# Early modulation groups as column strips, x loaded ahead of the parameter rows

## What is computed

```
cs = jax.nn.silu(c)
for l in range(DEPTH):
    mod = cs @ P['w_mod'][l] + P['b_mod'][l]            # (2, 1024) @ (1024, 6144)
    sh1, sc1, g1, sh2, sc2, g2 = jnp.split(mod[:, None, :], 6, axis=-1)
    hn = _rms_norm(x, P['norm_mix_g'][l]) * (1.0 + sc1) + sh1
    y = mixer(hn, ...)                                  # begins with hn @ w_in
    x = x + g1 * y
    hn = _rms_norm(x, P['norm_ffn_g'][l]) * (1.0 + sc2) + sh2
    x = x + g2 * _swiglu(hn, P['w_ffn_in'][l], P['w_ffn_out'][l])
y = _rms_norm(x, P['final_norm_g'])
```

## Time and profile before

| | us |
|---|---|
| median of three runs | 1574.86 (1574.68 to 1576.28) |
| the profiled execution | 1577.25 |
| its span, first to last instruction | 1575.7 |
| PE busy in the span | 1456.3 (92%) |
| first projection matmul starts | 80.4 |

### The profile page before, as it was taken

The page is one execution under the profiler, slowest core; times in us unless marked ns, Lnnn a source line. Parts: engine busy times, 40 slices in busy tenths (PEclk is TensorE's granted clock), DMA queues, the critical chain, the costliest instruction groups (busy, mean ns, idle before and its releaser), DMA issues.

```text
span 1575.7 us, 28758 instructions
## 1 busy us (share of the span) xinstructions
PE 1456.3 (92%) x11021; PEld 1387.6 (88%) x11021; DVE 911.6 (58%) x1644; ACT 511.2 (32%) x763; POOL 128.9 (8%) x150
## 2 busy tenths in 40 slices
PE   5789999996999999999949999996979999999997
PEld 4789899796999999999939888885979999999997
DVE  3566567648886788378674447655463333333344
ACT  2135444424222222222343335443232212222233
POOL 0000000001221122012000000000001100100100
PEclk9999999997999999999969899998989999999998
DMA  8324334342554455345212131230312323233222
GB/s 257 133 81 141 114 124 125 111 137 91 173 163 147 147 161 161 107 137 162 67 40 56 35 85 52 71 93 18 93 54 80 93 87 87 80 94 93 81 74 77
DMA packets 230317, 164.67 MB, mean 105 GB/s; under 512 B 9990, under 2 KB 216520, under 8 KB 230100
## 3 DMA queue, kind: packets, MB, share of 16 engines
q1 hardware_dynamic: 217636, 118.47, 25.9%
q0 software_dynamic: 12288, 44.85, 8.6%
q10 hardware_dynamic: 304, 0.10, 0.0%
HBM read 159.80 MB, written 3.60 MB: 104 GB/s over the span
## 4 chain that ended last, share of the span: by engine, by line
PE 74%; DVE 12%; ACT 6%; issue 4%; DMA 3%; SPq 1%; POOL 0%; DVEq 0%; ACTq 0%; POOLq 0%
PE ring L606 64%; PE core_j L444 2%; ACT weight_high L416 1%; DVE weight_low L421 1%; DMA weight_raw<-in_c_w_in 1%; DMA mixer_area<-in_x_sample 1%; PE core_j L546 1%; PE core_k L1315 1%; PE ring L2144 1%; PE core_j L517 1%; DVE norm_rstd L616 1%; DVE norm_step L614 1%; DMA weight_raw<-in_a_w_in 0%; PE core_k L1318 0%; DVE norm_step L613 0%
## 5 line engine op out<-in xcount | busy, mean ns | idle before, releaser
L606 PE MATMUL ring<-normed_high,weight_high 128*128 128x272 f32 x2128 | 455.2, 296 | 42.7 <-DVE normed_low L698 27.3
L606 PE MATMUL ring<-normed_high,weight_low 128*128 128x272 f32 x2128 | 446.9, 292 | 0.0
L606 PE MATMUL ring<-normed_low,weight_high 128*128 128x272 f32 x2128 | 445.9, 291 | 0.0
L606 PEld LDWEIGHTS ring<-normed_high,weight_high 128*128 128x128 f32 x2128 | 341.3, 193 | 53.8 <-issue 45.5
L606 PEld LDWEIGHTS ring<-normed_low,weight_high 128*128 128x128 f32 x2128 | 341.5, 192 | 0.0
L606 PEld LDWEIGHTS ring<-normed_high,weight_low 128*128 128x128 f32 x2128 | 339.4, 193 | 0.0
L421 DVE TENSOR_TENSOR weight_low<-weight_raw,weight_high 128x1024 fp32r<-128x1024 f32 x197 | 257.3, 1306 | 72.1 <-ACT weight_high L416 70.6
L416 ACT ACTIVATE weight_high<-weight_raw 128x1024 fp32r<-128x1024 f32 x197 | 206.8, 1050 | 180.1 <-PE ring L606 156.2
L606 PE MATMUL ring<-mixed_high,weight_high 128*128 128x272 f32 x960 | 204.0, 294 | 17.9 <-DVE mixed_low L1992 7.4
L606 PE MATMUL ring<-mixed_high,weight_low 128*128 128x272 f32 x960 | 201.3, 292 | 0.0
L606 PE MATMUL ring<-mixed_low,weight_high 128*128 128x272 f32 x960 | 200.6, 291 | 0.0
(11 more groups left out here) (384 smaller groups left out, 1257.2 us busy)
## 6 DMA issues: line engine op xcount, KB each, us to landing
weight_raw<-in_w_ffn_in SPq DMA_DIRECT2D x88, 512.0 KB, 3.7
mod_weight<-in_w_mod POOLq DMA_DIRECT2D x48, 512.0 KB, 4.2
mod_weight<-in_w_mod POOLq DMA_DIRECT2D x18, 1024.0 KB, 5.7
weight_raw<-in_w_ffn_out SPq DMA_DIRECT2D x32, 512.0 KB, 3.6
weight_raw<-in_a_w_in SPq DMA_DIRECT2D x24, 512.0 KB, 4.0
weight_raw<-in_c_w_in SPq DMA_DIRECT2D x20, 512.0 KB, 3.8
mixer_area<-in_w_mod SPq DMA_DIRECT2D x6, 1024.0 KB, 12.4
weight_raw<-in_w_ffn_out SPq DMA_DIRECT2D x16, 384.0 KB, 3.2
```

What stands on the lines that cost most here:

```text
L606: last = pe.matmul(PS[p.slot][:, half, 0:HALF], w[n.slot][:, k, :], x[:, k, half * HALF:(half + 1) * HALF], start=(k == 0 and w is WH and ...
```

## The change

1. SP issues x and x_sample directly behind the identity (which now brings the two selector columns along), and the nine parameter rows behind them. All eight early groups go through SP's queue, in the order 0, 4, 1, 5, 2, 6, 3, 7, the first two projection weights behind the second. POOL loads group 8 and on.
2. The eight early groups are made as strips, in pairs, two groups to a bank of 512 columns, two banks in turn (`early_rows`). ACT copies a pair's rows out (`early_copy`), PE folds them by four matmuls (`early_fold`), and DVE adds the biases pair by pair (`early_read`). One pair makes sh1 and sc1 of two feature tiles.
3. The strips of the last pair and its fold stand between contraction tiles of the first two projections. Group 8's strips stand behind these.
4. ACT squares x as it was loaded, token-major, with the sum along the row. The reciprocal root is taken on 128x5 numbers, and PE spreads it over the partitions by five matmuls. DVE copies the transposed x out.
5. The norm's gain is made pair by pair, and the tiles of a pair directly behind it (`norm_gain`, `norm_tile`). DVE's softplus stands behind all of them.
6. SP's loop over the heads is written out.

The diff, cut to its core:

```diff
+        MG_ORDER = (0, 4, 1, 5, 2, 6, 3, 7)
...
+        def early_rows(pe, i):
+
+            if i >= 2:
+                pe.wait_ge(s_mrc, 2 * (i - 1))
+            for e in (2 * i, 2 * i + 1):
+                pe.wait_ge(s_early[e % EARLY_BUFS], 16 * (e // EARLY_BUFS + 1))
+                rows_of(pe, EARLY[e % EARLY_BUFS], EPS_ROWS[i % 2][:, 2 * P * (e % 2):2 * P * (e % 2) + 2 * P])
+
+        def early_fold(pe, i):
+            pe.wait_ge(s_mrc, 2 * i + 2)
+            if i >= 2:
+                pe.wait_ge(s_mod, 2 * (i - 1))
+            for n in range(4):
+                mm = pe.matmul(EPS_COLS[i % 2][:, 2 * n:2 * n + 2], EROWS[i % 2][:, n * P:(n + 1) * P], FOLD,
+                               start=True, stop=True)
+            mm.then_inc(s_modu, 2)
+
+        def rows_of(pe, w, dst):
+
             for k in range(KD):
                 q = slice(32 * (k % 4), 32 * (k % 4) + 32)
-                mm = pe.matmul(MRPS[q], CSW[:, k, :], MW[:, k, :], start=(k < 4), stop=(k >= 4))
+                mm = pe.matmul(dst[q], CSW[:, k, :], w[:, k, :], start=(k < 4), stop=(k >= 4))
             mm.then_inc(s_mrows, 1)
...
         def _(sp):
...
-            with sp.Fori(0, HEADS) as h:
+            for h in range(HEADS):
...
         def _(pool):
-            load_mod(pool, 0, lambda: MG_DIRECT)
...
-            pool.wait_ge(s_modu, 1)
-            load_mod(pool, 0, lambda: MG_DIRECT + 1)
-            pool.wait_ge(s_direct, MG_DIRECT)
+            pool.wait_ge(s_mrows, MG_NORM - 2)
+            load_mod(pool, 0, lambda: MG_NORM)
+            pool.wait_ge(s_modu, MG_NORM)
             for a in (XB[:, 0:PAD], XB[:, TC + PAD - 1:TC + PAD], GW[0], GW[1]):
                 ins = pool.memset(a, 0.0)
             ins.then_inc(s_clear, 1)
-            pool.wait_ge(s_modu, MG_NORM - MG_DIRECT)
-            load_mod(pool, 0, lambda: MG_NORM)
...
         def _(pe):
...
+            early_rows(pe, 0)
+            pe.wait_ge(s_add, KD)
+            p = Turn(R_N0)
+            pe.wait_ge(s_free[p.slot], p.before)
+            for b in range(NB):
+                pe.matmul(PS[p.slot][:, 0, b * P:(b + 1) * P], NR[:, b:b + 1].to_broadcast([P, P]), IDENT,
+                          start=True, stop=True)
...
+            early_fold(pe, 0)
+            early_rows(pe, 1)
+            early_fold(pe, 1)
+            early_rows(pe, 2)
+            early_fold(pe, 2)
...
+            for k in (0, 1):
+                first_two(k)
+            early_rows(pe, 3)
+            for k in (2, 3):
+                first_two(k)
+            early_fold(pe, 3)
+            for k in (4, 5, 6, 7):
+                first_two(k)
             pe.wait_ge(s_mod, MG_NORM)
             mod_rows(pe, MG_NORM)
...
         def _(act):
...
+            early_copy(act, 0)
+            act.wait_ge(s_squ, 1)
+            p = Turn(R_N0)
+            st.add(act.activation(NR[:, 0:TP], PS[p.slot][:, 0, :], ACT.Copy))
+            act.activation(NR[:, TP:T], PS[p.slot][:, 1, 0:TS], ACT.Copy).then_inc(s_free[p.slot], 1)
+            early_copy(act, 1)
+            norm_high(act, 0, 0, 0, 2)
+            early_copy(act, 2)
+            norm_high(act, 0, 0, 2, 4)
+            early_copy(act, 3)
+            norm_high(act, 0, 0, 4)
```

More of the change, by code:

```diff
@@ L50 @@
 GELU_A, GELU_B = 0.7978845608028654, 0.044715
-C_ID, C_COS, C_SIN = 0, P, P + T
+C_ID, C_SEL, C_COS = 0, P, P + 2
+C_SIN = C_COS + T
 C_DEC = C_SIN + T
@@ L432, in mod_source, with load_early @@
             return t["w_mod"][l].rearrange("(k p) m -> p k m", p=P)[:, :, ds(a0, 2 * P)]
[L434 to L450, removed]
+        def load_early(q, e):
+            if e >= EARLY_BUFS:
+                q.wait_ge(s_mrows, e - EARLY_BUFS + 1)
+            q.dma_start(EARLY[e % EARLY_BUFS], mod_source(0, MG_ORDER[e] * 2 * P)).then_inc(s_early[e % EARLY_BUFS], 16)
         def load_mod(pool, l, g):
@@ L479, in mod_parts @@
                     ins.then_inc(s_part, 1)
[L481 to L496, removed]
         def sum_parts(pe, acc, dst):
@@ L650, in norm_act, with norm_high @@
             act.activation(NR[:, :], NR[:, :], ACT.Exp, scale=-0.5).then_inc(s_r0, 1)
-        def norm_high(act, q, shift):
-            for k in range(KD):
+        def norm_high(act, q, shift, first=0, end=KD):
+            for k in range(first, end):
                 act.wait_ge(s_hf, KD * q + k + 1)
@@ L658, in norm_high, with norm_gain, norm_tile, norm_dve @@
                                bias=MOD[:, shift + k, 1:2]).then_inc(s_hnh, 1)
-        def norm_dve(dve, q, p, shift, scale, gain, rstd=True):
-            st = steps["dve"]
[L663 to L667, removed]
-            for k in range(KD):
[L669 to L672, removed]
-                st.add(dve.scalar_tensor_tensor(out=dst[:, 0:TP], in0=X[:, k, 0:TP], scalar=GAIN[:, k, 0:1],
-                                                in1=NR[:, 0:TP], op0=ALU.mult, op1=ALU.mult))
-                dve.scalar_tensor_tensor(out=dst[:, TP:T], in0=X[:, k, TP:T], scalar=GAIN[:, k, 1:2],
-                                         in1=NR[:, TP:T], op0=ALU.mult, op1=ALU.mult).then_inc(s_hf, 1)
+        def norm_gain(dve, scale, gain, k=0, n=KD):
+            steps["dve"].done(dve.scalar_tensor_tensor(
+                out=GAIN[:, k:k + n, :], in0=MOD[:, scale + k:scale + k + n, :], scalar=1.0,
+                in1=gain[:, k:k + n].unsqueeze(2).to_broadcast([P, n, 2]), op0=ALU.add, op1=ALU.mult))
+        def norm_tile(dve, q, k):
+            st = steps["dve"]
+            if KD * q + k >= 4:
+                dve.wait_ge(s_hnh, KD * q + k - 3)
+                dve.wait_ge(s_hnl, KD * q + k - 3)
+            dst = NORM_BUF[k % 4]
+            st.add(dve.scalar_tensor_tensor(out=dst[:, 0:TP], in0=X[:, k, 0:TP], scalar=GAIN[:, k, 0:1],
+                                            in1=NR[:, 0:TP], op0=ALU.mult, op1=ALU.mult))
+            dve.scalar_tensor_tensor(out=dst[:, TP:T], in0=X[:, k, TP:T], scalar=GAIN[:, k, 1:2],
+                                     in1=NR[:, TP:T], op0=ALU.mult, op1=ALU.mult).then_inc(s_hf, 1)
+        def norm_dve(dve, q, p, shift, scale, gain):
+            norm_gain(dve, scale, gain)
+            norm_rstd(dve, q, p)
+            for k in range(KD):
+                norm_tile(dve, q, k)
                 if k:
```

166 lines of the change are left out of this document (99 added, 67 removed).

## The result

The changed kernel took 1538.38 us (median of four runs, 1534.54 to 1540.98); the kernel before, measured beside it, 1575.57 (four runs, 1574.68 to 1576.63). The ratio is 0.9753, with a 95% interval of 0.973 to 0.9776: 37 us faster. The forecast was 1547.0 with a range of 1539 to 1558, so the measured time lies 0.6 us under the lower end, and the gain was larger than the sum of 27.8: by 9.4 us in these medians, by 10.7 in the two profiled executions. The profiled execution took 1538.78 (span 1537.2) against 1577.25 (span 1575.7) before: 38.5 less.

The account below looks back on a forecast made before the run. The prediction took the opening's serial chain, mostly PE's work up to group 9's strips, as the bound: strips 27.9 us earlier, 27.2 net, plus 0.6 for SP's loop, summed to 27.8, giving 1547.0 us, range 1539 to 1558.

Parts of the forecast that it names:

- x at 13.0: Opening: with x issued ahead of the rows, PE starts on x at 13.0 us; its eight tiles end at 23.3.
- the two-bank order without a hidden copy: Early strips: each fold stands directly behind its rows, so ACT's 0.8 us copy is hidden only for the first pair.
- the early loads hidden: Opening loads: the sixth group lands between 33 and 35 us, pair 2 wants it at 39.4; 4 us in hand.
- softplus hidden: Before the K rotation: DVE's 3.95 us of softplus; PE would still be ready 1.9 us before group 9's load.
- the new wait for group 9's load: Behind the first projections: load issued only after group 8's strips have read the buffer, landing at 70.1 us.
- the 0.65 lost there: Group 9's strips: they run at the low level, 0.65 us more, leaving 27.2 net of 27.9.
- Groups as strips: Early groups: eight at 1.93 us instead of five at 6.9 and three by DVE, all at the low level.
- products of tiles 0 and 1: First projections: 24 matmuls, 4.2 us of old time at the low level before the clock rises, 4.9 in all.
- the loop: Heads' ends: writing out SP's loop gains 0.6 us, at most 3.5.
- the second rival: Early strips: the clock rises during them, saving 3.9 us on three pairs and 2.0 on folds: 1541; chance 0.20.
- the start's lower bound: Opening: PE's start on x at 11.9 us, with the rows landing as before, instead of 13.
- The first rival: Opening: each of eight tiling mode changes costs its 0.63 us in full, 5 us: 1552; chance 0.10.

Follow-up runs that it names:

- the pause: Changed kernel with PE's first strips waiting for the first two projection weights' low parts, a pause of 3.44 us behind the x transposes; 1541.95 us.
- the run that rose in the last x transpose: Changed kernel with group 8's strips directly behind the fourth fold and DVE's softplus steps spread between the normed tiles; 1535.11 us.
- the old form: Changed kernel with only the strips undone: all eight early groups as two-column matmuls, in the new order, without row copies and folds; 1581.46 us, ratio 1.0044.

## Why the prediction missed

**Right.** x at 13.0 (13.18 measured) and its end at 23.3 (23.52); the two-bank order without a hidden copy (fold 1 waits 0.78 for ACT); the early loads hidden; softplus hidden; the new wait for group 9's load, issued 53.43 and landed 5.76 later, where 64.3 and 5.8 were forecast; the low level at group 9's strips (1.94) and the 0.65 lost there against the kernel before; the shift kept to the end.

**Wrong.** The step is "Groups as strips", in the sentence that all of it runs at the low level "as every PE row before 84 is", and the terms built on it. The prediction had named the sign itself: a strip group that takes much other than 1.93.

| term | forecast | measured | difference |
|---|---|---|---|
| first pair | 3.9 | 2.59 | -1.3 |
| second and third pair | 7.8 | 3.84 | -4.0 |
| broadcasts | 2.1 | 1.42 | -0.7 |
| folds 0 to 2 | 5.25 | 3.1 | -2.2 |
| products of tiles 0 and 1 | 4.9 | 3.11 | -1.8 |
| fourth pair, group 8 (forecast high) | 3.9 | 2.9 | -1.0 |
| everything else up to 59.33 | 42.25 | 42.4 | +0.1 |

The first five rows are 10.0 of the 10.8 us by which group 9's strips came earlier than forecast (59.33 against 70.1), and all five are the level, but for a few tenths of price (a pair that ran low throughout took 3.64 behind the pause, not 3.9). The sixth is a mis-sized price: 1.28 a group was read as the price of strips at the high level, but that row itself stood partly at the low one (granted clock 0.78 from 98.0 to 99.2). The measured price is 0.93 to 1.05. Outside this sum, the loop was worth 1.3 where 0.6 was forecast.

The time that came out is nearest to the second rival, the rise during the strips, at 1541. It had been given 0.20, on the ground that "transposes and columns ran at the low level from 17 to 69 without a rise". Here the reading failed: that stretch holds two kinds of work. The 10 us of transposes ended about where the rise comes in the runs that have something else behind them, and the two-column matmuls behind them took it away. The runs show the first (the extra transposes, and the run that rose in the last x transpose) and the second (the two-column records put back, and the fourth pair of the old form). Strips as such, the rival's cause, were not needed for it. The rival was also too small: it left a strip group at 1.28 where 0.96 was measured, and the broadcasts and the first products at the low price.

The range left too little room below. With the start's lower bound this rival gives 1539.9, and with the upper bound of the loop as well 1537; the lower end was put at 1539.

The first rival, a price for each mode change, falls: the second pair follows the first fold at 28.45 without a gap, and the broadcasts the first pair at 26.05. The Trainium skill, "TensorEngine Tiling (Array Packing)", Key Properties, states that a change of tiling mode drains the engine. The trace has little room for it at these places: the first eight broadcasts took 1.09 where eight such records took 0.89 elsewhere, and the products behind the fourth pair 3.20 where those behind a fold took 3.11, so some 0.1 to 0.2 us a change (an estimate). The 0.63 of idle weight load went by the level: behind strips it was 0.81 at the low level (61.19) and 0.41 at the high one (78.82), and the strips' own matmuls were running meanwhile.

What stays open: why the rise came at different points. In seven kernels whose opening is the same up to there, the changed one among them, the first pair took between 1.86 and 3.21 us; the first entry of granted clocks lies between 23.24 and 26.33.

## What to carry over

Before pricing new work at the level that the old trace shows, ask which kind of work kept TensorE there: here the two-column matmuls kept PE busy by every count for 34 us and yet ran at 1.2 GHz, and replacing them raised the pace of what stands behind them. That was the 10 us that the forecast lacked, and with the old form in the new order the whole gain was gone. And when a wait moves, look at what the released load has behind it: group 9's load, softplus, then weight 2 each became the next thing that was late.

## What the runs showed of the hardware

- Strips in four column groups overlap here: 32 records of 256 columns took 1.86 to 1.93 us at the high level, 0.06 each, where a product record of 272 columns on the full array took 0.13.
- Two-column matmuls at a full busy share ran at 0.215 us a record for 34 us before and for 41 in the experiment; where they began at the high level, the granted clock fell from 1.00 to 0.50 within the pair (0.65 over it).
- Transposes alone were followed by the rise to 2.4 GHz: 32 more of them took 4.33 us where 8.3 would have been the low pace, and in one run the last x transpose was already faster (0.25 against 0.31).
- The table's granted clock reads 1.00 in the opening while the pace doubles, because the trace has no entry before the first rise (24.98); it showed 0.50 only after the first fall. In the opening, go by durations.
- A load that ran beside others made them late: the rows landed at 14.84 with 1 MB beside them and at 12.94 without.
